# A transformer stack on one core: three changes of order in the mixer, two in the ScalarE stream and one in the VectorE stream

## The reference, cut to what matters

```python
    def block_fn(i):                                   # stick_breaking: 8 heads
        z = jnp.einsum('bhqd,bhkd->bhqk', qb, k).astype(jnp.float32) * scale
        log_rem = jnp.where(mask, jax.nn.log_sigmoid(-z), 0.0)
        suffix = lax.cumsum(log_rem, axis=3, reverse=True) - log_rem
        a = jnp.where(mask, jnp.exp(jax.nn.log_sigmoid(z) + suffix), 0.0)
        return jnp.einsum('bhqk,bhkd->bqhd', a, v)
...
    p_s = masked_softmax(jnp.einsum('bhgqd,bhqkd->bhgqk', qb, ksb) * scale, m_s)   # nsa_mixer: selected
    p_w = masked_softmax(jnp.einsum('bhgqd,bhkd->bhgqk', qb, kwb) * scale, m_w)    # and window attention
...
    return jax.nn.gelu(flat @ w1) @ w2                 # compress: keys and values of blocks of 32 tokens
...
x = x + jnp.concatenate([o_nsa, o_sb], axis=-1) @ w_out[l]
x = x + memory_cross_attention(rms_norm(x, mem_x_norm[l]), rms_norm(mem, mem_kv_norm[l]), mem_wq[l], mem_wk[l], ...)
```

## Time and profile before

| | |
|---|---|
| median of 3 runs | 1238.31 us (1237.34 to 1238.56) |
| the profiled execution | 1237.44 us, span 1235.7 us |
| TensorE matmul busy | 1211.3 us, 98% of the span |
| VectorE busy | 693.5 us, 56% |
| ScalarE busy | 545.5 us, 44% |
| DMA | 217.94 MB, mean 176 GB/s |
| mean granted TensorE clock | 0.99 of full speed |

### The profile page before, as it was taken

How to read it: one execution, slowest core, us unless ns; L and a number is a source line. 1 busy time by engine, 2 the same in 40 slices (tenths; PEclk the granted TensorE clock), 3 DMA queues, 4 the chain that set the end, 5 groups by cost and what they waited for, 6 DMA issues and landing times.

```text
span 1235.7 us, 14840 instructions
## 1 busy us (share of the span) xinstructions
PE 1211.3 (98%) x6191; PEld 1011.7 (82%) x6191; DVE 693.5 (56%) x706; ACT 545.5 (44%) x656; POOL 62.6 (5%) x122
## 2 busy tenths in 40 slices
PE   8999999999999999999999999999998988999998
PEld 6888888888889977888888888888977876888886
DVE  5667455555466755566546555546905876555452
ACT  5535344344355544534435444434527343444430
POOL 2100000000010001000001000003200010000000
PEclk9999999999999999999999999999999997999999
DMA  7754466655486318664646755645725314465550
GB/s 272 272 204 156 154 195 193 204 179 203 146 289 205 103 46 261 207 217 163 216 136 195 231 173 171 235 137 160 240 72 171 103 53 135 155 195 168 198 204 34
DMA packets 147699, 217.94 MB, mean 176 GB/s; under 512 B 5137, under 2 KB 115761, under 8 KB 147506
## 3 DMA queue, kind: packets, MB, share of 16 engines
q1 hardware_dynamic: 144658, 206.69, 50.7%
q0 software_dynamic: 2976, 10.31, 2.5%
HBM read 215.93 MB, written 1.05 MB: 176 GB/s over the span
## 4 chain that ended last, share of the span: by engine, by line
PE 94%; DVE 3%; ACT 1%; DMA 1%; issue 0%; POOL 0%; SPq 0%; DVEq 0%; POOLq 0%; ACTq 0%
PE acc L1737 28%; PE acc L1739 28%; PE acc L1738 28%; PE turn L1730 4%; PE acc L1940 1%; DVE w_lo L1107 1%; PE acc L2188 1%; DMA raw<-in_mem_wk 1%; ACT w_hi L759 1%; PE turn L2166 1%; PE turn L1865 1%; PE turn L1920 1%; DVE xt L1117 1%; PE turn L2051 0%; DMA raw<-in_a_w_in 0%
## 5 line engine op out<-in xcount | busy, mean ns | idle before, releaser
L1107 DVE TENSOR_TENSOR w_lo<-raw,w_hi 128x2048 fp32r<-128x2048 f32 x188 | 424.4, 2279 | 197.1 <-ACT w_hi L759 196.9
L1737 PE MATMUL acc<-w_hi,xt 128*128 128x512 f32 (+2 forms) x1112 | 436.2, 392 | 4.6 <-DVE xt L1117 2.4
L1739 PE MATMUL acc<-w_hi,xt 128*128 128x512 f32 (+2 forms) x1112 | 429.5, 386 | 0.0
L1738 PE MATMUL acc<-w_lo,xt 128*128 128x512 f32 (+2 forms) x1112 | 428.7, 386 | 0.0
L759 ACT ACTIVATE w_hi<-raw 128x2048 fp32r<-128x2048 f32 x188 | 353.0, 1906 | 149.4 <-PE acc L1739 121.3
L1737 PEld LDWEIGHTS acc<-w_hi,xt 128*128 128x128 f32 x1112 | 210.8, 190 | 48.2 <-issue 2.8
L1739 PEld LDWEIGHTS acc<-w_hi,xt 128*128 128x128 f32 x1112 | 210.3, 189 | 42.6
L1738 PEld LDWEIGHTS acc<-w_lo,xt 128*128 128x128 f32 x1112 | 210.8, 190 | 39.6
L804 ACT ACTIVATE sg<-acc,rstd 128x256 f32<-128x256 f32 x88 | 37.0, 471 | 240.5 <-PE acc L1739 240.5
L1737 PE MATMUL acc<-w_hi,ht 128*128 128x512 f32 x352 | 139.6, 397 | 0.0
L1739 PE MATMUL acc<-w_hi,ht 128*128 128x512 f32 x352 | 138.0, 392 | 0.0
(11 more groups left out here) (259 smaller groups left out, 842.1 us busy)
## 6 DMA issues: line engine op xcount, KB each, us to landing
raw<-in_ffn_w_gate_up SPq DMA_DIRECT2D x88, 512.0 KB, 5.1
raw<-in_ffn_w_down SPq DMA_DIRECT2D x22, 1024.0 KB, 5.0
raw<-in_ffn_wg SPq DMA_DIRECT2D x44, 512.0 KB, 4.1
raw<-in_ffn_wu SPq DMA_DIRECT2D x44, 512.0 KB, 5.1
raw<-in_ffn_wd SPq DMA_DIRECT2D x22, 1024.0 KB, 5.1
raw<-in_a_w_in SPq DMA_DIRECT2D x15, 1024.0 KB, 6.7
raw<-in_w_in SPq DMA_DIRECT2D x10, 1024.0 KB, 5.2
raw<-in_a_w_out SPq DMA_DIRECT2D x8, 1024.0 KB, 5.2
```

Of the source, the lines that this page charges most:

```text
L1107: V.tensor_tensor(w_lo[:, u % RING, 0:kt * w], raw[:, raw_at["unit", u], 0:kt * w], w_hi[:, u % RING, 0:kt * w].bitcast(F32), ALU.subtract ...
L1737: mm(o, lhs[0], rhs[0], start=start, stop=False)
L1738: mm(o, lhs[0], rhs[1], start=False, stop=False)
L1739: return mm(o, lhs[1], rhs[0], start=False, stop=stop)
```

## The change

Three steps move; no instruction is added, removed or resized, and TensorE's, SP's and GpSimd's streams stay as they are. On ScalarE `stick_weights(1)` goes ahead of the high part of `mem_wk`, and the gelu goes behind the high part of `U_MOUT`. On VectorE `shift2(0)` goes ahead of the low part of `mem_wk`, and `shift2(1)` ahead of `stick_low(1)`.

```diff
@@ ScalarE
             stick_high(0)
             stick_logs(1)
+            stick_weights(1)
             split_to(U_MIN + 13)
-            stick_weights(1)
             act.wait_ge(s_cused, N_CW)
             nc.scalar.activation(hidp[:], acc[0][:].rearrange("p (i m) -> p i m", i=2), ACT.Copy).then_inc(s_cpart, 1)
             exps2(0)
             stick_high(1)
             split_to(U_MIN + 14)
             exps2(1)
+            split_to(U_MOUT + 1)
             act.wait_ge(s_turned, N_CHT + 1)
             turned_hid = tb[N_CHT % 4]
             nc.scalar.activation(hid[:].rearrange("p m n -> p (m n)"), turned_hid[:, 0:64], ACT.Gelu_apprx_tanh)
...
             last.then_inc(s_afree, 1)
-            split_to(U_MOUT + 1)
             exps2(2)
@@ VectorE
             copy_bank(N_HEADS + 2, kkt[:].rearrange("p k n -> p (k n)"))
             stick_low(0)
-            split_to(U_MIN + 13)
...
             shift2(0)
+            split_to(U_MIN + 13)
+            shift2(1)
             stick_low(1)
-            shift2(1)
             split_to(U_MIN + 14)
             shares2(0)
             split_to(U_MOUT + 1)
```

## The result

| | before | after |
|---|---|---|
| median | 1237.82 us (4 runs, 1236.93 to 1238.56) | 1231.49 us (4 runs, 1229.81 to 1232.39) |
| profiled execution | 1237.44 us, span 1235.7 | 1229.81 us, span 1228.1 |

The ratio is 0.9948 with a 95% interval of 0.9930 to 0.9965. The medians are 6.3 us apart, the profiled executions 7.6 us. The forecast was 6.6 us, and 1231.3 us. The interval alone, 4.3 to 8.7 us saved, fits most of the rivals as well (5.1, 5.6 and 8.0 saved); what tells them apart is the trace.

What follows compares the result with a forecast made beforehand. TensorE, holding 94% of the chain, was taken as the bound; a 5.03 us stall and 1.50 us of slow clock, 6.6 us at `turned_hidden`, gave 1231.3 us, the middle of 1230.8 and 1231.7. The range was 1229.4 to 1234.0.

Steps and rivals of the forecast that it cites:

- the rivals: Clock falls anyway, 5.1 us saved (0.12); later fall goes away, 8.0 (0.10); wait moves to `mem_wk`'s low part, 5.6 (0.08).
- The chain and the sum: TensorE holds 94% of the chain; with stall and slow clock gone, `turned_hidden` starts 6.6 us earlier, at 936.6.
- The stall: TensorE stands 5.03 us ahead of `scores2(0)`, until ScalarE, itself waiting for `mem_wk`, frees the banks; it goes.
- The slow clock behind it: `scores2(0)` took 3.16 us against 1.66 for `scores2(1)` with the same shapes; 1.50 us go with the stall.
- What is late next: `memory_product(0, 0)` needs `mem_wk`'s low part, done at 932.3, some 0.2 us before TensorE comes; costed at nothing.
- `exps2(0)` would be held with VectorE's old order: Old order gives the low part at 931.6 but the maxima at 933.3, with `exps2(0)` behind them.
- The cover of the low part: `mem_wk`'s low part ends some 0.2 us before TensorE comes; each microsecond of landing beyond about 928 costs one.
- The parts at nothing: Swapping `shift2(1)` and `stick_low(1)` is worth nothing; the output weight's earlier low part 0 to 0.2 us, taken as 0.
- The load of the Exp table: On ScalarE, 1.28 us behind the sums of head 0 at 921.7; first two banks free at 923.8.
- The clock rival in the packed stretch: Clock falls anyway among the small matmuls from 919 to 932.5; 1.50 us lost again, 5.1 saved; chance 0.12.
- The rival of the later fall: The clock's fall at 965 to 970 goes away, worth some 1.5 us; 8.0 us saved; chance 0.10.
- One sign that the prediction gave for being wrong: A shift that is 6.6 us at 937 and shrinks behind it.

Runs made afterwards that it cites:

- the filled kernel: 20 more matmuls of 128x512 ahead of `scores2(0)` on the kernel before, filling TensorE's idle time; 1233.50 us, ratio 0.9977.
- the third profile of before: The kernel before, unchanged, profiled a third time; 1238.70 us, one run.
- ScalarE's move alone: Only the stick weights put ahead of the high part of `mem_wk`, on the kernel before; VectorE's order and the gelu stay; 1232.84 us, ratio 0.9975.
- the kernel with the later low part: The changed kernel with the low part of `mem_wk` one step later on VectorE, behind `shift2(1)`; 1235.81 us, ratio 0.9991 to the kernel before.
- the repeat: The changed kernel run again without alteration, beside the kernel without the gelu's move; 1229.84 us, ratio 0.9931 to the kernel before.

## Why the prediction was right

**The chain and the sum.** The stall hung on the order in ScalarE's stream, and its size was read right: 5.03 forecast, 5.10 found at `scores2(0)`. The slow clock behind it was priced at 1.50; 1.41 were found at `compressed_unit(3)` (6.51 - 5.10), and the filled kernel shows the same 1.49 by itself. That price was read from one execution, and here there was luck. Beside the third profile of before, where the slow clock lasts 6.8 us, L2111 of the changed kernel is 7.7 us ahead (946.03 - 936.00, less 2.30 for the turns near 835): 1.4 us more of slow clock, less the 0.3 us wait for ScalarE, which it covers. The change takes away the stall and whatever slow clock follows it; 6.6 us is the smaller of the two sizes seen.

**What is late next.** 6.63 us at L2111 is what the sum gave. The prediction said that `exps2(0)` would be held with VectorE's old order; ScalarE's move alone shows it, with 3.96 us instead of 6.63. The cover of the low part was thin but enough; the kernel with the later low part shows that behind it each microsecond counts, and more than one for one.

**The parts at nothing.** The gelu behind the output weight and the swap are worth nothing, in the times and in the traces.

**Where a term was off.** The load of the Exp table was put behind the sums of head 0. It ran at 918.69, ahead of them, so the first two banks were free at 922.5 (923.1 on the times of before) and not at 923.8; both are before TensorE asks, and nothing hung on it. The clock rival in the packed stretch didn't come: 1.00 from 919 to 940 in the profile of after. The rival of the later fall was right as a mechanism: the fall near 966 was longer in the first profile after, missing in the second, and missing in the two kernels without the gelu's move; it moves an execution by about 1.5 us either way. In the kernel before it was 3.4 us long, 6.8 and missing in three profiles, so the change isn't needed to move it.

One sign that the prediction gave for being wrong did come: in the first profile the shift shrinks behind 937, to 4.97 at `values2(3)` just ahead of 976. The cause is this fall and no new wait; in the second profile, without it, the shift doesn't shrink. The prediction took that fall as the only loose one behind the stall; the falls in the memory attention are loose as well and moved the gain by 2 us. So the total was partly luck: the order of work gave 6.6, the falls behind it took 1.7 and gave 2.0 back, and the repeat came out at 8.5 us. The 7.6 us between the profiled executions are 6.63 at L2111, 0.4 from these falls, and 0.63 from ahead of the change.

## What to carry to other kernels

Where an engine waits for a transfer, look at what stands behind the wait in its stream and doesn't need it; but follow the freed engine to its next releaser before counting the gain, since here 2.7 of 6.6 us would have been lost to a stall that the first one had covered. The 5 us stall of TensorE cost more than its length: add the difference between what the matmuls behind it take at either clock, and look at more than one profile before pricing that, since the slow stretch was 3.4 us long in two profiles of before and 6.8 in the third. Compare two traces by the starts of the same step, less their difference ahead of the change; with that a tenth of a microsecond could be read here where the times scatter by 2 us or more, up to the place where the clock falls differently.

## What the runs showed of the hardware

Repeated profiles of the same program differ in where the clock falls, also where TensorE shows no idle time: near 966 the kernel before had 3.4 us of half speed in one profile, 6.8 in the next and none in the third. Much of the scatter of the times goes with the clock: in the 29 runs of before, nine of the ten with a mean clock of 0.992 took 1234.7 to 1236.1 us (the tenth 1238.9), the twelve with 0.990 1236.8 to 1238.3.

Filling 5 us of idle time with 20 useless matmuls made the kernel 2.8 us faster (1.5 to 4.2). The trace shows 1.5 us of that: the clock didn't fall behind the idle time. The rest isn't shown.

An ACT_TABLE_LOAD doesn't always wait for what its ACTIVATE waits for: the one of L969 ran at 918.69, while its first ACTIVATE waited for the sums until 921.12, but that of L963 came after 2.08 us of idle time, when the scores (L2053) were done. In the kernel with the later low part the load of the gelu ran at 941.68 and its ACTIVATE waited for TensorE until 945.39. Why the load of L963 came late isn't shown.
